# The second attention's weights as running products: values multiplied by parts, two heads side by side on TensorE

## The reference, cut to what matters

```python
def block(args):
    i, qb = args
    qpos = i * QB + jnp.arange(QB)
    mask = kpos[None, :] < qpos[:, None]
    z = jnp.einsum('bhqd,bshd->bhqs', qb, k).astype(jnp.float32) * scale
    log_beta = jax.nn.log_sigmoid(z)
    log_1mb = jnp.where(mask, jax.nn.log_sigmoid(-z), 0.0)
    suffix = lax.cumsum(log_1mb, axis=3, reverse=True) - log_1mb
    a = jnp.where(mask, jnp.exp(log_beta + suffix), 0.0)
    return jnp.einsum('bhqs,bshe->bhqe', a.astype(v.dtype), v)
...
o = o.reshape(b, s, SB_W) * jax.nn.silu(g)
return x + o @ w_out
```

## Time and profile before

| | |
|---|---|
| times of 3 runs | 2392.08, 2392.08, 2384.33 us; median 2392.08 |
| the profiled execution's own time | 2385.55 us |
| its span | 2383.7 us |
| PE, DVE, ACT busy over the span | 2301.2 (97%), 1592.2 (67%), 1017.9 us (43%) |
| chain that ended last | PE 80%, DVE 11%, ACT 6% |
| granted TensorE clock | 0.997 |

### The profile page before, as it was taken

How to read it: one execution, slowest core, us unless ns; L and a number is a source line. 1 busy time by engine, 2 the same in 40 slices (tenths; PEclk the granted TensorE clock), 3 DMA queues, 4 the chain that set the end, 5 groups by cost and what they waited for, 6 DMA issues and landing times.

```text
span 2383.7 us, 30315 instructions
## 1 busy us (share of the span) xinstructions
PE 2301.2 (97%) x12762; PEld 1234.2 (52%) x12762; DVE 1592.2 (67%) x2053; ACT 1017.9 (43%) x1482; POOL 208.1 (9%) x254
## 2 busy tenths in 40 slices
PE   7999999999999999999999988999999999989999
PEld 5445444444444444445544456654444446777765
DVE  6888867866766666787632389965534406989961
ACT  6255334322323223433322587732313216888841
POOL 0001030000000001623301100022000000000000
PEclk9999999999999999999999999999999999999999
DMA  5111010111110212103111000111231200010021
GB/s 187 36 37 69 1 36 36 61 46 71 58 49 36 71 71 71 38 1 142 36 71 36 32 5 1 62 46 36 71 141 36 72 1 1 1 36 1 1 89 54
DMA packets 50488, 116.02 MB, mean 49 GB/s; under 512 B 2418, under 2 KB 8107, under 8 KB 49968
## 3 DMA queue, kind: packets, MB, share of 16 engines
q1 hardware_dynamic: 48616, 105.40, 12.4%
q10 hardware_dynamic: 1736, 8.68, 0.9%
HBM read 101.49 MB, written 12.58 MB: 48 GB/s over the span
## 4 chain that ended last, share of the span: by engine, by line
PE 80%; DVE 11%; ACT 6%; issue 1%; DMA 1%; SPq 0%; DVEq 0%; ACTq 0%
PE PS L72 76%; PE PS L75 4%; ACT RG L81 3%; DVE R L93 2%; DVE RG L107 2%; ACT OV L84 2%; DVE R L101 1%; DVE RG L104 1%; DVE RG L101 1%; DVE RG L93 1%; ACT R L81 1%; DMA RG<-in_a_w_in 1%; DVE oss L110 1%; DVE dg L104 1%; DVE scl L110 0%
## 5 line engine op out<-in xcount | busy, mean ns | idle before, releaser
L72 PE MATMUL PS<-R,RG 128*128 128x512 f16 (+1 forms) x5184 | 1104.2, 374 | 9.4 <-DVE R L101 4.2
L72 PEld LDWEIGHTS PS<-R,RG 128*128 128x128 f16 (+1 forms) x5184 | 514.0, 104 | 592.8 <-issue 10.9
L72 PE MATMUL PS<-RG,R 128*128 128x512 f16 (+1 forms) x2904 | 631.2, 377 | 2.0 <-DVE R L101 1.7
L72 PEld LDWEIGHTS PS<-RG,R 128*128 128x128 f16 x2904 | 283.7, 98 | 330.0 <-issue 2.9
L81 ACT ACTIVATE RG<-RG,scl 128x4096 f16<-128x4096 f32 (+2 forms) x70 | 177.9, 2557 | 199.5 <-DVE scl L113 199.5
L101 DVE SCALAR_TENSOR_TENSOR RG<-RG,scl 128x4096 f16<-128x4096 f32 (+2 forms) x70 | 213.1, 3051 | 71.5 <-ACT RG L81 71.5
L101 DVE SCALAR_TENSOR_TENSOR R<-PS,scl,R 128x512 f32<-128x512 f32 (+1 forms) x227 | 159.2, 742 | 121.2 <-PE PS L72 98.8
L81 ACT ACTIVATE R<-PS,scl 128x512 f32<-128x512 f32 (+1 forms) x128 | 83.5, 685 | 326.4 <-PE PS L72 287.0
L107 DVE TENSOR_TENSOR_SCAN RG<-RG 128x127 f32<-128x127 f32 (+7 forms) x128 | 168.4, 1343 | 76.3 <-ACT RG L81 76.1
L110 DVE TENSOR_REDUCE scl<-RG 128x1 f32<-128x4096 f32 (+1 forms) x35 | 150.3, 4293 | 98.9 <-DMA RG<-in_w_ff 41.1
L72 PE MATMUL PS<-R,OV 128*128 128x64 f32 (+2 forms) x1456 | 193.7, 274 | 5.7 <-DVE R L93 5.4
(11 more groups left out here) (137 smaller groups left out, 1667.2 us busy)
## 6 DMA issues: line engine op xcount, KB each, us to landing
RG<-in_w_ff SPq DMA_DIRECT2D x16, 2048.0 KB, 8.5
RG<-in_a_w_in SPq DMA_DIRECT2D x8, 2048.0 KB, 8.7
xspill<-R ACTq DMA_DIRECT2D x2, 4096.0 KB, 16.0
RG<-in_w_kv SPq DMA_DIRECT2D x4, 2048.0 KB, 8.2
RG<-in_b_w_in SPq DMA_DIRECT2D x4, 2048.0 KB, 8.1
RG<-in_w_in SPq DMA_DIRECT2D x3, 2048.0 KB, 8.2
R<-in_x SPq DMA_DIRECT2D x8, 512.0 KB, 8.0
RG<-in_w_out SPq DMA_DIRECT2D x2, 2048.0 KB, 7.8
```

Source lines behind the costliest of these rows:

```text
L72: return self.engine.matmul(*a, **k) if self.engine else Nothing()
```

## The change

1. The mask moves from TensorE into the scan: `later` (bf16, in `dg`) holds 1 at masked places of the last square and 0 before, and the scan computes max(product, later), so the running product is 1 up to the diagonal. The 128 mask matmuls are gone, and each scan covers one column more.
2. One sigmoid, sigmoid(-z), per group; the second sigmoid and the join are gone. The scan's result is transposed as it is.
3. `turned` is now an `activation` (Copy, scale -1, bias 1): it writes 1 - p.
4. The values are replaced by their differences before the attention: for each 128 tokens two DMAs issued by ScalarE bring V2 shifted by one token into OV, and VectorE subtracts, one tile per `q2` product.
5. The multiplication is turned round: 64 columns of the difference are the stationary side, the turned square (128 columns, fp32) streams. An even head writes partitions 0 to 63 and an odd one 64 to 127, and their matmuls alternate (`values`). The output has features on partitions; so `g2` is made by `product_t`, and `gate_turn` is gone.
6. Order: `sb_steps` has one group per step for i below 4 and two from 4 (54 steps). A step's scores are issued one or two steps ahead, its halves are turned in that step and multiplied in the next. There are two PSUM places for scores instead of three, two for transposes, two for outputs.
7. The scale of the split comes from a matmul with `ones` (`gate_bound`) instead of GpSimd. Buffers move; weight tiles 40 and 41 exchange their places.

```diff
+        V2_BEFORE = [OV[:, 1024 * i:1024 * i + 1024] for i in range(2)]
+        LEFT = [RG[:, 12288 + 1024 * i:13312 + 1024 * i] for i in range(4)] + [RG[:, 4096:5120]]
+        TURNED = [OV[:, 0:1024], OV[:, 1024:2048], RG[:, 6144:7168], RG[:, 7168:8192]]
...
+        later = dg[:, :, :].rearrange("p t q -> p (t q)").bitcast(BF16)
...
+        def left(u):
+            return LEFT[u % 5]
+
+        def turned_at(u):
+            return TURNED[u % 4]
...
+        HG = R3[:, 0:8192].bitcast(F16).rearrange("p (t g s k q) -> p t g s k q", t=8, g=2, s=2, k=4)
...
+        sb_steps = [[u] for u, (i, _) in enumerate(sb_groups) if i < 4]
+        sb_steps += [[u, u + 1] for u in range(len(sb_steps), len(sb_groups), 2)]
...
-            for t in range(NT - 1):
-                for c in range(2):
-                    product_n(38 + c, t, ("g2", t, c), bank=6 + c if t == NT - 2 else None)
...
+            for z, key in enumerate(G2[:14]):
+                _, c, mi, n = key
+                product_t(38 + c, mi, n, h_rhs, key, bank=z - 6 if z >= 12 else None)
...
+            def gate_bound(first, last, bank):
+
+                key = ("gate_bound", first)
+                b = banks.take_at(key, bank)
+                e.wait_ge(*sig("g_peak").at(last - 1))
+                e.wait_ge(*banks.free(key))
+                e.matmul(b[:, first:last], ones[:, :], col(24 + first, last - first), start=True,
+                         stop=True).then_inc(*full.up(*key))
...
-                                e.matmul(z[:, q:q + n], Q2[pr, a, h // 2, 128 * i:128 * i + 128],
-                                         K2[pr, b, h // 2, q:q + n], start=(a + b == 0), stop=(a == 1))
-                    for u, i, h, z in pair:
-                        mm = e.matmul(z[:, w - 128:w], identb[:, :], maskb[:, :], start=False, stop=True,
-                                      skip_group_check=True)
...
+                                mm = e.matmul(z[:, q:q + n], Q2[pr, a, h // 2, 128 * i:128 * i + 128],
+                                              K2[pr, b, h // 2, q:q + n], start=(a + b == 0), stop=(a == 1))
+                                if (a, q + n, two + 2) == (1, w, len(items)) and (len(groups) == 2 or h % 2):
+                                    mm.then_inc(*full.up("zb", u))
...
+            def turn(u, s):
+
+                _, at, n = sb_halves(u)[s]
+                b = banks.take_at(("tb", u, s), 4 + sb_units.index((u, s)) % 2)
+                e.wait_ge(*sig("scanned").at(u))
+                e.wait_ge(*banks.free(("tb", u, s)))
+                for x in range(0, n, 128):
+                    mm = e.transpose(b[:, x:x + 128], left(u)[:, at + x:at + x + 128], ident[:, :])
+                mm.then_inc(*full.up("tb", u, s))
+
+            def values(step):
+
+                pairs = []
+                for u in step:
+                    i, hs = sb_groups[u]
+                    pairs += [(u, x, h) for x, h in enumerate(hs)]
+                pairs = list(zip(pairs[:len(pairs) // 2], pairs[len(pairs) // 2:]))
+                return [(u, i, x, h, j) for two in pairs for j in range(i + 1) for u, x, h in two]
+
+            def multiply(work):
+                for u, i, x, h, j in work:
+                    g = h // 8
+                    if h % 8 == 0 and j == 0:
+                        banks.take_at(("pvb", i, g), 6 + g)
+                        e.wait_ge(*banks.free(("pvb", i, g)))
+                        e.wait_ge(*sig("v_steps").at(0))
+                    at = width(i) * x + 128 * j
+                    e.wait_ge(*sig("turned_b").at(u, at // 512))
+                    r, q = 64 * (h % 2), 128 * (h % 8 // 2)
+                    mm = e.matmul(banks.ap(("pvb", i, g))[r:r + 64, q:q + 128], V2[:, j, 64 * h:64 * h + 64],
+                                  turned_at(u)[:, at:at + 128], start=(j == 0), stop=(j == i))
+                    if j == i and h % 2:
+                        mm.then_inc(*full.up("pvb", i, h))
...
-                            mm = e.matmul(banks.ap(("pvb", i, g))[:, 64 * (h % 8):64 * (h % 8) + 64],
-                                          AT2[v % 2][:, at:at + 128], V2[:, j, 64 * h:64 * h + 64],
-                                          start=(j == 0), stop=(j == i))
...
+            product_t(39, 3, 1, h_rhs, G2[15], bank=7)
+            ahead = [[u] for u in range(3, 22)] + sb_steps[22:]
+            for z, step in enumerate([*sb_steps, []]):
+                if step and (0 < z < 20 or z > 20) and ahead:
+                    scores(ahead.pop(0))
+                if step == sb_steps[-1]:
+                    gate_bound(0, 7, 0)
+                work = values(sb_steps[z - 1]) if z else []
+                units = [(u, s) for u in step for s in range(len(sb_halves(u)))] or [None]
+                for y, unit in enumerate(units):
+                    if unit:
+                        turn(*unit)
+                    multiply(work[len(work) * y // len(units):len(work) * (y + 1) // len(units)])
...
-            gate_turn(0)
-            gate_turn(1)
...
+                    if (c, t) == (0, 1):
+                        gate_bound(7, 8, 5)
...
-                        product_n(40 + c, t, ("fo", t, c))
-                    if c == 0 and t + 2 < NT:
-                        gate_turn(t + 2)
+                        product_n(40 + c, t, ("fo", t, c), lhs=g_lhs)
...
+                    if 8 * c + z in v_steps:
+                        t = v_steps[8 * c + z]
+                        if t == 0:
+                            e.memset(V2_BEFORE[0][0:1, :], 0.0).then_inc(*step.up())
+                            e.wait_ge(*step.last())
+                        e.wait_ge(*sig(f"v_before{t % 2}").at(t))
+                        e.tensor_tensor(V2[:, t, :], V2[:, t, :], V2_BEFORE[t % 2], ALU.subtract).then_inc(
+                            *sig("v_steps").up(t))
...
+            e.memset(later[:, 0:896], 0.0)
             e.wait_ge(*sig("mask_in").at())
-            e.tensor_copy(maskb[:, :], OV[:, 2048:2176]).then_inc(*sig("constants").up("mask_s"))
+            e.tensor_copy(later[:, 896:1024], OV[:, 2048:2176]).then_inc(*step.up())
...
+            def gate_factors(first, last):
+
+                key, n = ("gate_bound", first), last - first
+                e.wait_ge(*full.at(*key))
+                power(col(63 + first, n), col(40 + first, n), banks.ap(key)[:, first:last], key=key).then_inc(
+                    *sig("g_factor").up(first))
...
-                    e.wait_ge(*sig("one_minus").at(u))
-                    for x in range(n):
-                        back = kept(u)[:, w * x + 1:w * x + w][:, ::-1]
-                        scan = e.tensor_tensor_scan(back, back, back, 1.0, ALU.mult, ALU.bypass)
-                    scan.then_inc(*step.up())
-                if u < N:
-                    i, hs = sb_groups[u]
-                    w = width(i)
-                    eb, ec = by_head(EB[u % 4], u)[:, :, 0:w - 1], by_head(kept(u), u)[:, :, 1:w]
-                    e.wait_ge(*sig("beta").at(u))
-                    e.wait_ge(*step.last())
-                    e.tensor_tensor(eb, eb, ec, ALU.mult).then_inc(*sig("joined_b").up(u))
...
+            def scan(u):
+                i, hs = sb_groups[u]
+                w = width(i)
+                e.wait_ge(*sig("one_minus").at(u))
+                for x in range(len(hs)):
+                    back = left(u)[:, w * x:w * x + w][:, ::-1]
+                    last = e.tensor_tensor_scan(back, back, later[:, 1024 - w:1024][:, ::-1], 1.0, ALU.mult, ALU.max)
+                last.then_inc(*sig("scanned").up(u))
...
+            gated(sb_steps[-3])
+            gated(sb_steps[-2])
+            gate_factors(0, 7)
+            gate_low(0)
+            gate_low(1)
+            gated(sb_steps[-1])
...
+                    if 8 * c + z + 1 in v_steps:
+                        t = v_steps[8 * c + z + 1]
+                        before, done = V2_BEFORE[t % 2], sig(f"v_before{t % 2}")
+                        e.wait_ge(*sig("bank_act").at("v2", 1, NT - 1))
+                        e.wait_ge(*sig("h_low").at("b_norm_2", 1, 7))
+                        if t < 6:
+                            e.wait_ge(*sig("v_steps").at(t + 2))
+                        if t:
+                            e.dma_start(before[0:1, :], V2[127:128, t - 1, :]).then_inc(*done.up(t, 0, by=16))
+                        e.dma_start(before[1:128, :], V2[0:127, t, :]).then_inc(*done.up(t, by=16))
...
+            def turned(u, s):
+
+                _, at, n = sb_halves(u)[s]
+                e.wait_ge(*full.at("tb", u, s))
+                if u >= 4:
+                    i, hs = sb_groups[u - 4]
+                    e.wait_ge(*full.at("pvb", i, hs[-1] | 1))
+                else:
+                    e.wait_ge(*sig("v_steps").at(0))
+                e.activation(turned_at(u)[:, at:at + n], banks.ap(("tb", u, s))[:, 0:n], ACT.Copy, bias=1.0,
```

(30 more changed lines are left out.)

251 lines of the change are left out of this document (79 added, 172 removed).

## The result

Before 2390.69 us (median of 4 runs, 2384.33 to 2392.08), after 2455.08 us (4 runs, 2452.39 to 2457.59): **ratio 1.027, 95% interval 1.025 to 1.030**. The prediction had 2308 us, 2276 to 2374, and 0.05 on slower. The error is 147 us, and the sign is wrong.

What follows compares the result with a forecast made beforehand. VectorE was taken to set the pace before, TensorE after (210.8 us plus 5 of waits). The last stage starting 75.0 us earlier plus 5.3 saved in it made 80.3 us less: 2305.2 or 2311.8, so 2308, range 2276 to 2374.

Steps and rivals of the forecast that it cites:

- Hidden parts, at nothing: Before the attention: eight value subtractions and their copies, 8.0 us each, fit in VectorE's idle 28 us and cost nothing.
- Rival 5: Attention loop: waits between the three engines in the new order eat the gain, about 2385 us; chance 0.02.
- TensorE's switches: Attention loop: 398 changes between whole array and halves of rows or columns, 0.093 us each, 37.0 us in all.
- rival 1: Attention loop: the 290 switches to or from halves of columns are free, 2284 us; chance 0.20.
- Two heads by columns: Value multiplications: an even and an odd head run in the time of one, 288 x 2 x 0.115 = 66.2 us.
- Rivals 2 and 3: Value multiplications: 2, heads don't overlap by columns, 2370 us, chance 0.16; 3, weight loads exposed, 2434 us, chance 0.05.
- The scan: VectorE in the attention: max and a bf16 second operand cost no time; one more column costs 0.3 us in all.
- Rival 4: VectorE in the attention: the scan with max takes half as long again, 2359 us; chance 0.03.
- Where the loop starts: Attention loop: starts at 1992.4 us, the same place in both programs.
- Last stage: After the attention: first product 75.0 us earlier, six products shorter by 0.88, 5.3 us; seventh's 1.8 us delay stays.
- The clock: TensorE's granted clock, 1.00 in the attention before, was expected not to change.
- The sum: Whole kernel: 75.0 + 5.3 = 80.3 us less, giving 2305.2 or 2311.8, forecast 2308 us.

Runs made afterwards that it cites:

- e1: Kernel after, with each shifted value copy of 127 partitions issued as two, of 112 and 15: 2342.8 us.
- e2: Kernel after, with the eight shifted copies each cut into partitions in a different way, one left whole at 127: 2357.5 us (one run).
- e9: e3 with the shifted copies cut in 122 and 5 partitions: 2353.8 us.
- e3: Kernel after, with VectorE's low half of each piece of weight tile 40 made one step after ScalarE's high half: 2434.9 us.
- e8: e1 with ScalarE making the high half of each piece of weight tile 40 at the beginning of its step, before the evictions: 2320.1 us.
- e4: Kernel after with the edits of e1 and e3 together: 2321.7 us.
- e5: e4 with the value matmuls of even and odd heads not in turn, all of one head and then the other: 2366.1 us.
- e10: e6 with ScalarE scaling the first tile's gates earlier and VectorE gating the last heads before splitting the second tile's gates: 2288.7 us.
- e7: e3 without shifted copies, VectorE subtracting zeros, so the output is another function's: 2320.2 us.
- e6: e4 with TensorE transposing two halves and then doing two shares of values, instead of one and one: 2291.2 us.

## Why the prediction was wrong, point by point

- **The step that failed**: "Hidden parts, at nothing". The copy was priced by `R<-in_x`, 8.0 us for 512 KB, because the bytes agree. That row has 128 partitions, the copy 127. On one engine a tile's copy takes 19.9 us, not 8.0. At 8.0 the eight would have held VectorE for 24 us, within its idle time; at 19.9 they take 160 us, and cost 112 (e1). No bound was kept for it: the "up to 10 us" stood for ScalarE's waits ahead of its evictions, not for the transfer, which was given no end above 8.0. How many partitions the copy has, and so how many engines carry it, was not asked.
 The Trainium skill, DMA: Bandwidth & Descriptors, "Why a DMA increments its semaphore by 16 and not by 1", has the rule: a DMA uses the largest number of engines up to 16 that divides the outermost dimension of both its sides, so 127 partitions go on one. By that rule one engine carries all of a copy here, and the trace agrees (share 0.06; e2, e9).
- **A step that was not there**: the low halves of weight tile 40. The prediction counted them as 6 us of VectorE's work and did not follow what the wait ahead of them is queued behind: about 20 us (e3, e8). Rival 5 had "waits between the three engines", with 0.02 and without naming this place.
- **TensorE's switches**, 0.093 us each: the switch measured 0.203 against 0.109, as taken, and of the new kind too (rival 1 falls). But the second slot after it is longer also: in e4 0.164 where transposes take 0.109, 0.160 from one pair of values to the next where later ones take 0.109. The 344 switches to transposes or values cost 0.053 more each, 18 us. The loop takes 236.6 us in e4, where 215.8 were forecast. The 0.093 was read from rows where only the first slot could be seen. That it is the change between whole array and halves, and not just between transposes and values, shows before, where both use the whole array and, where nothing is waited for, the first slot of either is 0.109 to 0.111. Four transposes go by in 0.44 us there (2225.42 to 2225.86) and in 0.58 after:

```profile
2224.48 1.10 PE L72 MATMUL PS<-R,OV 128*128 128x64 f32 x8
2225.42 0.61 PE L75 MATMUL PS<-ident,RG 128*128 128x128 f32 x4
```

 This compares two kernels; no run changes the tiling alone. The Trainium skill, TensorEngine Tiling (Array Packing), Key Properties, says that a change of mode drains TensorE; the longer slots agree with that, and put 0.15 us on it here.
- **Two heads by columns**: right, 0.109 us a pair against 0.115 taken. Rivals 2 and 3 fall (e5; a pair's slot is 0.109 us, where rival 3 had 0.167 for each record). But not all 576 records find a partner: 496 do in e4, so the values take 1152 - 496 = 656 slots of 0.109, 71.5 us where the sum has 66.2. With the 18 us of the switches this is more than the loop's 20.8, and the 5 us that the sum had for waits were not all needed.
- **The scan**: right (1346 against 1343 ns). Rival 4 falls.
- **Where the loop starts**: the forecast kept 1992.4; in e4 it is 1986.9. The mask matmuls between the 60 scores ahead of it are gone, 2.8 us (the first 48 take 1.45 us instead of 3.83), and these scores start 2.7 us earlier than before (1974.24 against 1976.93), which was not followed up. 5.5 us to the good.
- **Last stage**: products every 5.62 us, right. The 1.8 us of the seventh product, left as they are in the prediction, went. The start came 3.1 us after the last multiplication, not 1.1: the product's bank is freed by a gating that stands behind 2.7 us of splitting (e10).
- **The clock**: no change was expected. Its mean over the span is 0.975 after, 0.997 before and 0.999 in e4, so it came back when the two holes went.
- **The sum**, with the two causes away: 2303.4 + 20.8 - 5.5 + 2.0 - 1.8 = 2318.9 for e4's span of 2319.2. The four corrections are themselves read from e4's trace, so this shows that nothing large is left over, and it confirms no forecast. e4's 2321.7 us lies in the range, 14 above the forecast. So the range was right for the idea, and wrong for the program. The chance of slower stood on one mechanism in TensorE; the two that decided were a transfer and a queue, the first in a part that the text called hidden, the second in work that it counted for its length alone.

## What to carry to other kernels

Before a DMA is called hidden, price it by a row of its own shape, partitions first: a tile's copy took 19.9 us as 127 partitions and 3.6 as 112 and 15. When two engines' halves of a job move into the same step, write down what each half is queued behind; 0.75 us of work can tie the step into a ring. When an order alternates between ways to divide the array, group equal work: each change cost 0.15 us here, more than a slot of 0.109. Where two heads share the array, cut the work so that no record is left without its partner.

## What the hardware showed unexpectedly

- Two other transfers took far longer beside the copies on one engine. The issues of 1840 to 2025 us, before:

```profile
RG<-in_b_w_in SPq DMA_DIRECT2D x1, 2048.0 KB, 8.1
...
OV<-in_c_ms ACTq DMA_DIRECT2D x1, 64.0 KB, 1.9
```

 and after:

```profile
RG<-in_b_w_in SPq DMA_DIRECT2D x1, 2048.0 KB, 20.9
...
OV<-in_c_ms ACTq DMA_DIRECT2D x1, 64.0 KB, 18.3
```

 A mask of 64 KB took 18 us to land, while the DMA share was 0.06. It was issued on ScalarE's queue behind the last copy and landed at 2018.8, as that copy's subtraction began (2018.7). The weights come by another queue, and land in 20.9 us here and 11.7 in e1. With copies on two engines (e9) the two take 8.2 and 20.6 us. That they share an engine, or a queue, with the copies is my reading.
- TensorE's first product after the attention stands behind the same wait of 2.45 us in eight traces. In after, e1, e2 and e9 it takes 7.03 us with a granted clock of 0.76; in e3, e4, e7 and e8 it takes 5.34 with 1.00. In e6 it takes 7.03 after 2.06 us. So the length of the wait alone does not tell whether the clock falls behind it; why was not tried.
